# Every weight chunk fetched as two half-size transfers that signal one semaphore

## The chip, the cores and the metric

The kernel runs on one core of a Trainium2 chip. A core has TensorE (PE; its weight loads are listed as PEld), VectorE (DVE), ScalarE (ACT), GpSimd (POOL), and SyncE (SP), which in this kernel issues nearly all loads. Sixteen DMA engines move the data. The metric is the device time of one execution in microseconds; lower is better.

## The reference

Two blocks of two layers each, in f32, on 256 tokens (and 256 context tokens) of width 1024. The first block's layers are a modulated norm, an attention, and a mixture of experts; the second block's layers are attentions over latents and compressed keys, and a dense feed-forward of width 4096. What matters here is the weights that have to come in from HBM, and above all the experts:

```
def expert_block(args):
    xb, e = args
    return (jax.nn.silu(xb @ w1[e]) * (xb @ w3[e])) @ w2[e]
```

There are 32 experts in each of the two layers, w1 and w3 are 1024 x 512 and w2 is 512 x 1024 for each expert, so that one expert has 6 MiB of weights in f32, and one layer 192 MiB. The kernel fetches the weights of every expert, whatever the routing chose.

## The kernel before

**Chunks and places.** Weights come in chunks, mostly of 1 MiB: 128 partitions by 2048 floats, 8 KiB in each partition. `slot_at` names 20 places for a chunk: 6 in `ring`, and others in `rows`, `gate`, `arena`, `X` and `hT` at times when these hold nothing else. Each place has its own semaphore, `loaded[slot]`. SP runs the whole list of chunks in the order in which they are needed. For each it takes the next place (`Slots.take`), waits on the semaphore `used` until TensorE is done with the chunk that had the place before, and issues one DMA in `load` (line 3007), which adds 16 to `loaded[slot]` when it has landed. TensorE's `weights` (line 2168) waits for `loaded[slot]`, by a `Tally` that counts in units of 16.

**What a chunk is in HBM.** For w1 and w3 of an expert, partition p holds the rows 8p to 8p+7, each of 512 floats, and a chunk is four of these rows; for w2 it holds the rows 4p to 4p+3 of 1024 floats and a chunk is two of them. So each partition's 8 KiB of an expert chunk lie together in HBM, and the transfer is 128 pieces of 8 KiB, eight for each DMA engine. Chunks of `cols512` (the other projections, `w_mod`, `w_ff1_2`) are 4 x 128 pieces of 2 KiB, and chunks of `rows256` (`w_ff2_2`) are 2 x 128 pieces of 4 KiB.

**The experts.** `experts(l)` goes through 16 pairs of experts, 12 chunks to a pair: j = 0 to 3 are the chunks of w1, 4 to 7 those of w3, 8 to 11 those of w2 (even and odd expert in turn). The first pairs go to the places of `LEAD_PLACES`, all later ones to the 12 places of `STEADY_PLACES`, so 12 chunks are the most that are in flight or in use. Ahead of j = 11 of the first pair SP also stores the rows of the tokens (`h_rows`, line 3047), waits for the table that POOL scatters to HBM, loads it (line 3053), and waits until DVE has read it (`slots_ready`). For each further pair POOL gathers the tokens' rows with an indirect DMA (line 564), which moves on the same 16 DMA engines. On TensorE a pair is `up` twice (line 2689, w1 then w3), sums for the tokens of the pair before (line 2699), and the product with w2 (line 2730).

Of the kernel before, what the change touches and what calls it, by code (L numbers as in the profile page):

```python
# [170 lines left out]
def build(nc, t):  # L171
# [7 lines left out]
    with ctx:  # L179
# [3 lines left out]
        def sem(name):  # L183
            return ctx.enter_context(nc.semaphore(name))
# [129 lines left out]
        def slot_at(i):  # L314

            if i < RING:
                return ring[:, i, :]
            if i < 8:
                return rows[:, 2 * (i - RING):2 * (i - RING) + 2, :].rearrange("p a n -> p (a n)")
            if i < 10:  # L320
                return gate[:, i - 8, :, :].rearrange("p a n -> p (a n)")
            if i < 12:
                return arena[:, 12288 + CHUNK * (i - 10):12288 + CHUNK * (i - 9)]
            if i < 14:
                return X[:, 2 * (i - 12):2 * (i - 12) + 2, :].rearrange("p a n -> p (a n)")
            if i == 14:
                return hT[:, 4:8, :].rearrange("p a n -> p (a n)")
            at = {15: 10240, 16: 15360, 17: 6144, 18: 2048, 19: 4096}[i]
            return arena[:, at:at + CHUNK]
# [5 lines left out]
        loaded = [sem(f"loaded{i}") for i in range(20)]  # L335
# [257 lines left out]
        def _(act):  # L593
# [174 lines left out]
            def heads_ab():  # L768
                for j in range(12):
                    cols = slice(P * (j % 4), P * (j % 4) + P)  # L770
                    b = AB[j // 4]
                    act.wait_ge(mm_a, jobs.next())
                    bank = next_bank()
                    _, nq, q0 = b["q"]
                    inst = act.activation(qT[:, q0:q0 + nq, cols], bank[:, 0:P * nq].rearrange("p (h n) -> p h n", h=nq), ACT.Copy)
                    if b["k"]:
                        g0 = b["k"][1]
                        inst = act.activation(kD[:, g0:g0 + 2, cols], bank[:, 256:512].rearrange("p (g n) -> p g n", g=2), ACT.Copy)
                    inst.then_inc(a_free, 1)
                    act.wait_ge(a_free, so_far(a_free))  # L780
# [1352 lines left out]
        def _(pe):  # L2133
            v_done, a_done = Tally(v_free), Tally(a_free)
            fetched = [Tally(s, 16) for s in x_fetched]
            vi, ai, slots = [0], [0], Slots()
            chunk_in = [Tally(s, 16) for s in loaded]
            xn_in, rws, outs, picks = Tally(xn_ready), Tally(rows_ready), Tally(att_o), Tally(pick_ready)
            expd, tv, ta = Tally(att_e), Tally(att_tv), Tally(att_ta)
            mixed, choice, x_done = Tally(mod_row), Tally(chosen), Tally(x_tile)  # L2140
# [855 lines left out]
        def _(sp):  # L2996
# [3 lines left out]
            def load(src):  # L3000

                slot, before = slots.take()
                if before is not None:
                    freed.n = before + 1
                    sp.wait_ge(used, freed.value())
                dst = slot_at(slot)[:, 0:src.shape[1] * src.shape[2]].rearrange("p (k n) -> p k n", k=src.shape[1])
                sp.dma_start(dst, src).then_inc(loaded[slot], 16)

            def tokens():

# [3 lines left out]
            def matrix(w, cols, first=0):  # L3014
                for c in range(first, cols):
                    for src in cols512(w, c):
                        load(src)
# [7 lines left out]
            def experts(l):  # L3025

                def chunk(pair, j):

                    expert = bass.ds(2 * pair + j % 2, 1)
                    if j < 8:  # L3030
                        load(rows_of(t["w1" if j < 4 else "w3"][l, expert], KB, 4 * (j // 2 % 2), 4))
                    else:
                        load(rows_of(t["w2"][l, expert], 4, 2 * ((j - 8) // 2), 2))
# [189 lines left out]
```

## Time and profile before

| | |
|---|---|
| Median of 3 runs | 2365.07 us (2363.0 to 2366.71) |
| The profiled execution: its time | 2367.21 us |
| The profiled execution: its span | 2365.4 us |
| PE busy | 2205.4 us, 93% of the span |
| DVE busy | 957.6 us, 40% |
| Loads issued by SP and ACT | 595.26 MB, 64.3% of the 16 DMA engines' span |
| DMA, mean over the span | 255 GB/s |

The span is the time from the first to the last instruction. A share of busy time is an average over stages with different limits: DMA is busy 64% of the time because it is saturated in some stages and nearly idle in others. A row of the chain of work is one step on the way back from the last instruction to what released it.

### The profile page before, as it was taken

How to read it: one execution, taken by the hardware profiler on the slowest of the kernel's cores; microseconds unless marked ns; L12 is line 12 of the kernel's file. 1: busy time of each engine (PE TensorE's matmuls, PEld its weight loads, DVE VectorE, ACT ScalarE, POOL GpSimd, SP SyncE). 2: the span in 40 equal slices, each digit the busy share in tenths (PEclk: the TensorE clock that was granted, in tenths of full speed). 3: DMA queues.
4: the chain of work that ended last, by engine and by line, in shares of the span. 5: the costliest groups of instructions: out<-in, count | busy, mean ns of one | idle time of the engine just before them, and what ended most of it. 6: DMA issues, size and time to landing. Idle time of an engine off the chain costs nothing.

```text
span 2365.4 us, 25900 instructions
## 1 busy us (share of the span) xinstructions
PE 2205.4 (93%) x9574; PEld 1111.5 (47%) x9574; DVE 957.6 (40%) x1803; ACT 346.3 (15%) x941; POOL 158.4 (7%) x206
## 2 busy tenths in 40 slices
PE   6989999999999999989998888889999999999998
PEld 2436554333333344455333333334768744567843
DVE  3567433344333456273222222224630345561245
ACT  2006221000000010061000000001520001341000
POOL 1210002000000002030100000000000000000000
PEclk9999999999999999999999999999999999999999
DMA  9673348999999962206999999993324444504432
GB/s 374 244 277 145 126 178 321 420 421 421 421 421 421 422 233 71 71 1 232 382 420 420 421 421 421 421 409 121 124 71 144 150 171 136 181 25 133 163 143 98
DMA packets 150763, 602.98 MB, mean 255 GB/s; under 512 B 12660, under 2 KB 25716, under 8 KB 101136
## 3 DMA queue, kind: packets, MB, share of 16 engines
q1 hardware_dynamic: 145264, 595.26, 64.3%
q0 software_dynamic: 4736, 5.99, 0.7%
q8 instruction: 60, 0.98, 0.2%
q10 hardware_dynamic: 672, 0.49, 0.1%
q14 instruction: 31, 0.25, 0.0%
HBM read 606.89 MB, written 4.72 MB: 259 GB/s over the span
## 4 chain that ended last, share of the span: by engine, by line
PE 54%; DMA 29%; DVE 10%; issue 2%; POOL 2%; ACT 2%; SPq 1%; DVEq 0%; ACTq 0%; POOLq 0%
DMA ring<-in_w 14%; DMA arena<-in_w 13%; PE psum L2903 9%; PE psum L2262 9%; PE psum L2925 7%; PE psum L2689 7%; PE psum L2176 4%; PE psum L2784 4%; PE psum L2351 2%; PE psum L2730 2%; PE psum L2699 2%; DMA rows<-in_w 1%; POOL rstd L483 1%; PE psum L2431 1%; PE psum L2470 1%
## 5 line engine op out<-in xcount | busy, mean ns | idle before, releaser
L2689 PE MATMUL psum<-ring,arena 128*64 128x512 f32 x1440 | 326.5, 596 | 40.7 <-DMA ring<-in_w 38.8
L1689 DVE TENSOR_TENSOR X<-X,psum 128x512 f32<-128x512 f32 x192 | 131.9, 687 | 290.2 <-PE psum L2699 290.0
L2689 PEld LDWEIGHTS psum<-ring,arena 128*64 128x64 f32 x1440 | 105.8, 137 | 254.0 <-issue 243.5
L2262 PE MATMUL psum<-ring,hT 128*128 128x512 f32 x512 | 223.2, 593 | 1.9 <-DVE hT L1465 0.7
L2903 PE MATMUL psum<-hT,ring 128*128 128x256 f32 x1024 | 221.5, 379 | 2.6 <-DVE hT L1808 2.6
L2903 PEld LDWEIGHTS psum<-hT,ring 128*128 128x128 f32 x1024 | 194.4, 190 | 29.3 <-DVE hT L1808 3.0
L2699 PE MATMUL psum<-arena 128*128 128x512 f32 x384 | 178.3, 601 | 0.0
L2176 PE MATMUL psum<-con,arena 128*128 128x128 f32 (+1 forms) x848 | 123.7, 287 | 29.9 <-DVE arena L1776 10.6
L2262 PEld LDWEIGHTS psum<-ring,hT 128*128 128x128 f32 x512 | 95.8, 190 | 117.4 <-issue 115.1
L2176 PEld LDWEIGHTS psum<-con,arena 128*128 128x128 f32 (+1 forms) x848 | 96.7, 145 | 86.3 <-issue 25.0
L1776 DVE TENSOR_TENSOR arena<-psum,arena 128x512 f32<-128x512 f32 x32 | 33.8, 1058 | 209.2 <-PE psum L2689 209.2
L2730 PE MATMUL psum<-arena 128*64 128x512 f32 x488 | 112.3, 595 | 0.8 <-DVE arena L1780 0.8
L2699 PEld LDWEIGHTS psum<-arena 128*128 128x128 f32 x384 | 68.0, 190 | 88.1 <-issue 86.5
L2730 PE MATMUL psum<-gate,arena 128*64 128x512 f32 x232 | 105.1, 596 | 0.9 <-DVE arena L1780 0.9
L481 POOL TENSOR_SCALAR rstd<-sumsq 128x8 f32<-128x8 f32 (+3 forms) x44 | 10.7, 243 | 1372.8 <-ACT rows L618 419.8
L2784 PE MATMUL psum<-ring,hT 128*128 128x512 f32 (+2 forms) x256 | 94.6, 525 | 3.2 <-DVE gate L1930 2.7
L954 ACT ACTIVATE arena<-psum 128x512 f32<-128x512 f32 x32 | 19.1, 597 | 527.0 <-PE psum L2689 527.0
L2925 PE MATMUL psum<-ring,arena 128*128 128x512 f32 x192 | 88.1, 593 | 3.0 <-DVE arena L2012 3.0
L943 ACT ACTIVATE arena<-psum 128x512 f32<-128x512 f32 x64 | 38.2, 597 | 342.2 <-PE psum L2176 323.0
L2010 DVE TENSOR_SCALAR arena<-psum 128x512 f32<-128x512 f32 x16 | 11.1, 691 | 186.6 <-PE psum L2903 186.6
L2262 PE MATMUL psum<-arena,hT 128*128 128x512 f32 x192 | 84.3, 593 | 1.8 <-DVE hT L1115 1.8
L2689 PE MATMUL psum<-rows,arena 128*64 128x512 f32 x288 | 72.1, 592 | 0.0
(365 smaller groups left out, 2722.3 us busy)
## 6 DMA issues: line engine op xcount, KB each, us to landing
ring<-in_w SPq DMA_DIRECT2D x186, 1024.0 KB, 24.0
arena<-in_w SPq DMA_DIRECT2D x83, 1024.0 KB, 23.0
ring<-in_w_ff SPq DMA_DIRECT2D x64, 1024.0 KB, 5.9
rows<-in_w SPq DMA_DIRECT2D x50, 1024.0 KB, 23.8
ring<-in_w_mod SPq DMA_DIRECT2D x32, 1024.0 KB, 13.3
gate<-in_w SPq DMA_DIRECT2D x31, 1024.0 KB, 21.3
hT<-in_w SPq DMA_DIRECT2D x19, 1024.0 KB, 21.5
X<-in_w SPq DMA_DIRECT2D x15, 1024.0 KB, 24.2
```

What stands on the lines that cost most here:

```text
L943: act.activation(xgT[:, b, 4 * h:4 * h + 4, :], psum[:, 5 + h, :].rearrange("p (k n) -> p k n", k=4), ACT.Copy).then_inc(a_free, 1)
L1689: dve.tensor_tensor(x, x, bank, ALU.add).then_inc(v_free, 1)
L1776: dve.tensor_tensor(act_by_quarter, quarters(bank), quarters(siluG), ALU.mult).then_inc(v_free, 1)
L2176: return pe.transpose(out, in_, ident)
L2262: inst = pe.matmul(bank, hT[:, k, P * m:P * m + P], w[k], start=k == 0, stop=k == KB - 1)
L2351: inst = pe.matmul(bank, hT[:, 4 * h + i, P * m:P * m + P], w[c][:, i, :], start=i == 0, stop=i == 3)
L2689: inst = pe.matmul(out[64 * e:64 * e + 64, :], xgT[:, b, k, 64 * e:64 * e + 64], m, start=k == 0, stop=k == KB - 1)
L2699: pe.matmul(bank, shareT[:, m, :], ySlot[:, 512 * h:512 * h + 512], start=True, stop=True).then_inc(mm_v, 1)
L2730: inst = pe.matmul(outs[h][64 * e:64 * e + 64, :], actT[:, f, 64 * e:64 * e + 64], m, start=f == 0, stop=f == 3)
L2784: inst = pe.matmul(bank[:, 0:n], hT[:, k, P * m:P * m + P], w[k // 4][:, k % 4, :], start=k == 0, stop=k == KB - 1)
L2903: inst = pe.matmul(bank[:, SEQ * f:SEQ * f + SEQ], w[k][:, at:at + P], hT[:, k, 0:SEQ], start=k == 0, stop=k == KB - 1)
L2925: return pe.matmul(psum[:, PRODUCTS[n], :], a, b, start=i == 0, stop=i == 15)
```

## The change

`load` issues two DMAs in place of one. Each moves half of the chunk to its half of the same place, and both add 16 to the same semaphore, so TensorE's tally counts in units of 32 and waits until both have landed. A chunk with several rows to a partition is cut between its rows (for an expert chunk: 4 KiB and 4 KiB of each partition's 8 KiB), one with a single row to a partition (`w_kv_up_2`) in the middle of the row. The order of the chunks, their places and the wait for `used` are the same; the loads that don't go through `load` (tokens, parameters, the table, gates, the stores, and the rounds of `late`) are not touched.

```
-            chunk_in = [Tally(s, 16) for s in loaded]
+            chunk_in = [Tally(s, 32) for s in loaded]
...
                 if before is not None:
                     freed.n = before + 1
                     sp.wait_ge(used, freed.value())
+                k, n = src.shape[1:]
                 dst = slot_at(slot)[:, 0:src.shape[1] * src.shape[2]].rearrange("p (k n) -> p k n", k=src.shape[1])
-                sp.dma_start(dst, src).then_inc(loaded[slot], 16)
+                halves = [(slice(0, k // 2), slice(0, n)), (slice(k // 2, k), slice(0, n))]
+                if k == 1:
+                    halves = [(slice(0, 1), slice(0, n // 2)), (slice(0, 1), slice(n // 2, n))]
+                for r, c in halves:
+                    sp.dma_start(dst[:, r, c], src[:, r, c]).then_inc(loaded[slot], 16)
```

On SP, at the head of the loop over two pairs of experts, before: each row with DMA is one chunk of w1, and the register instructions between them work out its address and the value to wait for.

```order
L3061 ISA
L3007 ISA
L3007 DMA ring<-in_w 128x2048
L3005 REGISTER_ALU
L3007 ISA
L3007 DMA ring<-in_w 128x2048
L3005 REGISTER_ALU
```

The same place of SP after the change, the same two chunks.

```order
L3066 ISA
L3012 ISA
L3012 DMA ring<-in_w 128x1024
L3012 ISA
L3012 DMA ring<-in_w 128x1024
L3005 REGISTER_ALU
L3012 ISA
L3012 DMA ring<-in_w 128x1024
L3012 ISA
L3012 DMA ring<-in_w 128x1024
L3005 REGISTER_ALU
```

Each chunk has two DMAs of 128 pieces of 4 KiB where it had one of 128 pieces of 8 KiB, and for w1 one more register instruction; nothing has changed its place, and the instructions of the other engines are the same as before.

## Rows read from the trace of the kernel before

**Rows 1.** The page: busy times, and the span in 40 equal slices.

```profile
PE 2205.4 (93%) x9574; PEld 1111.5 (47%) x9574; DVE 957.6 (40%) x1803; ACT 346.3 (15%) x941; POOL 158.4 (7%) x206
...
DMA  9673348999999962206999999993324444504432
GB/s 374 244 277 145 126 178 321 420 421 421 421 421 421 422 233 71 71 1 232 382 420 420 421 421 421 421 409 121 124 71 144 150 171 136 181 25 133 163 143 98
```

**Rows 2.** Chain of work, both expert stages: start us, us, what.

```profile
381.36 14.03 DMA ring<-in_w
...
707.24 25.99 DMA ring<-in_w
733.37 3.68 PE psum L2689 x16
737.74 25.98 DMA ring<-in_w
...
1523.84 25.60 DMA arena<-in_w
1549.57 3.68 PE psum L2689 x16
1553.59 25.66 DMA arena<-in_w
```

**Rows 3.** Waits of PE on transfers, whole span: us in total, times, longest.

```profile
PE psum L2689 <- DMA ring<-in_w: 38.8, 38, 1.6
PE psum L2182 <- DMA ring<-in_w_mod: 14.6, 1, 14.6
...
PE psum L2689 <- DMA arena<-in_w: 10.0, 13, 1.0
...
PE psum L2689 <- DMA rows<-in_w: 0.8, 1, 0.8
```

**Rows 4.** Stretches: busy us of each engine, clock, DMA share, GB/s.

```profile
384.00:764.00 380.00, 368.11 (x1534) 134.62 (x1532) 148.25 (x197) 21.50 (x36) 23.79 (x25) 1.00 1.01 421
...
1142.00:1587.00 445.00, 399.12 (x1728) 141.70 (x1725) 99.74 (x148) 25.69 (x43) 23.37 (x24) 1.00 1.01 420
```

**Rows 5.** DMA packets at 800 to 830 us, expert chunks alone.

```profile
DMA packets 1734, 12.63 MB, mean 421 GB/s; under 512 B 192, under 2 KB 192, under 8 KB 192
...
q1 hardware_dynamic: 1733, 12.62, 101.1%
```

**Rows 6.** DMA packets at 1928 to 1932 us, chunks of w_ff2_2 alone.

```profile
DMA packets 422, 1.66 MB, mean 416 GB/s; under 512 B 16, under 2 KB 16, under 8 KB 422
...
q1 hardware_dynamic: 422, 1.66, 101.1%
```

**Rows 7.** DMA packets at 16 to 28 us, pieces of 2 KiB alone.

```profile
DMA packets 2349, 4.65 MB, mean 387 GB/s; under 512 B 80, under 2 KB 80, under 8 KB 2349
```

**Rows 8.** Shorter stretches: w_ff2_2 chunks, then expert chunks that follow idle DMA.

```profile
2308.50:2311.50 3.00, 3.00 (x9) 1.32 (x8) 2.90 (x5) 0.00 (x0) 0.00 (x0) 1.00 1.04 427
1103.00:1109.00 6.00, 5.39 (x40) 4.60 (x39) 1.73 (x4) 2.04 (x4) 0.00 (x0) 0.93 1.01 425
```

**Rows 9.** DMA issues, whole span: KB each, median us to landing.

```profile
ring<-in_w SPq DMA_DIRECT2D x186, 1024.0 KB, 24.0
...
ring<-in_w_in_c SPq DMA_DIRECT2D x12, 1024.0 KB, 6.6
...
ring<-in_w_out_c SPq DMA_DIRECT2D x4, 1024.0 KB, 5.0
```

**Rows 10.** SP in order of time, 500 to 531 us: issues of chunks.

```profile
500.72 0.84 SPq L3007 DMA_DIRECT2D ring<-in_w  x2
504.15 0.84 SPq L3007 DMA_DIRECT2D rows<-in_w  x2
511.46 0.33 SPq L3007 DMA_DIRECT2D gate<-in_w  x1
```

**Rows 11.** SP in order of time, start of layer 1's expert stage.

```profile
1096.45 1.28 SPq L3007 DMA_DIRECT2D ring<-in_w  x3
...
1131.74 0.33 SPq L3053 DMA_DIRECT2D arena<-slot_table  x1
1136.54 0.33 SPq L3007 DMA_DIRECT2D arena<-in_w  x1
```

**Rows 12.** Chain of work, last pairs of layer 0.

```profile
772.86 7.07 PE psum L2689 x32
...
802.78 7.07 PE psum L2689 x32
...
832.75 7.07 PE psum L2689 x32
```

**Rows 13.** Waits of SP, 384 to 1590 us.

```profile
SPq L3007 <- PE psum L2689: 394.4, 115, 7.8
```

**Rows 14.** Chain of work, start of the program.

```profile
13.29 14.62 DMA gate<-in_w_mod
27.91 2.80 issue
```

## The prediction

> **What bounds the kernel now.** I began with the page's slices. PE is busy 93% of the span, and yet in slices 8 to 14 and 20 to 27 the DMA engines are full, at a flat 420 to 422 GB/s [rows 1]. These are the two expert stages, and a flat top like this says that DMA may set the pace although PE is nearly always busy. The chain of work settles it. In layer 0 it has one wait of 26 us for a chunk in each pair of experts, with some 3.7 us of PE behind it, and the next such wait begins 30.5 us after the last (707.24 to 737.74) [rows 2]. In layer 1 the same goes on to 1553.59 + 25.66 = 1579.25 us. The 26 us are not the time of a transfer but of the queue ahead of it: the median chunk lands 24.0 us after its issue [rows 9], and a chunk takes some 2.49 us of all 16 engines (below), so about ten are queued. PE's own waits for these chunks are short, 38.8 + 10.0 + 0.8 us in all [rows 3], because the work of PE takes nearly as long as that of DMA: 368.11 of 380 us in layer 0, 399.12 of 445 us in layer 1 [rows 4]. So a longer chunk delays the end of an expert stage by nearly its full cost, and a shorter one would soon meet PE, above all in layer 0.
>
> Elsewhere PE waits for a transfer once, 14.6 us near the start [rows 3], where the queue is full too [rows 7, 14]. Nothing of the second block waits for a load.
>
> **What a 1 MiB chunk costs.** Three sizes of piece can be read, each in a stretch where the queue held nothing else. Time is stretch x 16 engines / data packets.
> - 8 KiB (experts before): 1734 packets in 30 us, 192 of them under 512 B (the writes to the semaphore, and a few more), so 30 x 16 / 1542 = 311 ns a piece [rows 5]. A chunk has 8 to an engine: 2.49 us.
> - 4 KiB: 422 packets in 4 us, 16 of them small, so 4 x 16 / 406 = 157.6 ns, and 16 to an engine make 2.52 us [rows 6].
> - 2 KiB: 2349 packets in 12 us, 80 small: 84.6 ns, and 32 to an engine make 2.71 us [rows 7].
>
> The middle one is what the change makes of an expert chunk, so by rows 5 and 6 the smaller pieces add 0.03 us. The second completion adds one small packet to each engine. Its price alone isn't in a row. Below, it is nothing, if it hides behind the data; above, I take what the line through the 2 and 8 KiB pieces leaves for a packet of no size, 84.6 - (311 - 84.6) / 3 = 9 ns. Together 0.04 us.
>
> How sure is this? From below: another stretch of 4 KiB pieces shows 427 GB/s in 3 us [rows 8], where whole packets at its edges weigh some 1%; if 4 KiB pieces ran at the 421 GB/s of the 8 KiB ones, only the completion would be left, 0.009 us. From above: the line through 2 and 8 KiB gives 84.6 + 75.5 = 160 ns for 4 KiB, a chunk of 2.56 us, and with the completion +0.08 to 0.09 us. One more comparison speaks for more: expert chunks that follow an idle queue run at 425 GB/s [rows 8], 2.47 us a chunk, and the 4 KiB rows are of that kind too; like with like the difference is 0.055 us, with the completion 0.06. I take 0.045 us, nearer to the longer stretches.
>
> The Trainium skill (DMA: Bandwidth & Descriptors, "Why small descriptors are slow (HBM only)") speaks against this change: each packet has a fixed overhead of about 3 cycles beside one cycle for 32 bytes. By that a chunk would grow from 8 x 259 to 16 x 131 cycles, 1.2%, an estimate of 0.03 us, and the time by some 10 us; this case's rows agree on the sign and leave the size between 0.009 and 0.09 us.
>
> **How many chunks it counts for.** In layer 0 the first pair comes piecemeal. SP works through the lead, and the chain turns to DMA at 381.36 us, with a chunk that lands at 395.39: j = 3 of the second pair, chunk number 15, since the chain repeats with each pair, and 737.74 + 25.98 = 763.72 is twelve pairs of 30.7 us later, chunk 159 [rows 2]. From 764 on the chain is PE's: the first products of a pair follow each other by 29.92 and 29.97 us [rows 12], and twelve chunks without gathers take 12 x 2.49 = 29.9 us. PE and DMA are level there to 0.1 us a pair; a slower DMA stays the limit until the last pair, chunk 183. From chunk 11 (the one that ends the idle time at about 378 us) to 183 are 172 to 173 chunks: 172 x 0.045 = 7.7 us, less 0.1 of slack.
>
> In layer 1 the queue fills at 1096 us [rows 11] and the lead counts as well: the table's load is issued at 1131.74 behind chunks still queued in the same queue, and what it releases begins at 1136.54. From chunk 3 to chunk 187 (j = 7 of the last pair, the last wait of the chain) are 185: 8.3 us. That PE has the chain up to 1187 us changes nothing, since the queue stays full beneath it at 420 GB/s [rows 4], and it is the queue that PE then meets.
>
> At the start seven chunks of `w_mod` precede the one wait [rows 14]. They have 2 KiB pieces before and after, so they gain only the completion: 7 x 0.009 = 0.1 us.
>
> **What costs nothing.** The other 160 or so chunks, behind PE's work: no wait of PE names them [rows 3], and one that lands 6.6 us after its issue [rows 9] would land a few hundredths later. Without that cover each would cost its 0.01 to 0.045 us, 7 us at most. SP issues twice as often. An issue takes 0.33 us and the two in a row 0.84 [rows 10], so 24 in a pair take 12 us of SP's 30.5. Behind a waiting issue stand all later loads, but SP waits for PE most of the time (394.4 us on line 2689 alone) [rows 13] and its issues run 24 us ahead of their landing. The second half is issued 0.5 us after the first, which needs 1.25 us to move, so no gap opens, not even for a lone chunk. There is no gain either: PE still waits for both halves, and nothing lands for it sooner.
>
> Sum: 7.7 - 0.1 + 8.3 + 0.1 = 16.0 us, 0.68%. The profiled execution took 2367.21 us, 1.8 more than its span; the median of the runs is 2365.07. The sum goes on the median: 2381 us.
>
> **The rivals.**
> - **Nothing to measure** (0.09): 4 KiB pieces cost the same for a byte as 8 KiB ones, as the 427 GB/s of rows 8 allow, and the completion hides or costs its 9 ns: 357 x 0.009 = 3 us, 2368. Against it: the 416 GB/s of rows 6, the longest such stretch.
> - **Twice the cost** (0.09): in the full queue, with HBM rows now 16 KiB apart and half used in each pass, a piece costs the line's 160 ns: 357 x 0.085 = 30 us, 2395. A kin of it is a shallower queue. If the queue held ten transfers and not ten chunks, it would hold 12.5 us of work. SP's longest wait in the stage is 7.8 us [rows 13], so it would still not run dry; only below three chunks would each pair lose time.
> - **Faster** (0.03): 4 KiB pieces stream better in the full queue than 8 KiB ones. The place is the queue in both stages, the price from the 427 GB/s: 2.456 us a chunk, and 9 ns more, 0.025 us less than now, so 357 x 0.025 = 9 us, 2356. (In layer 0 PE's 29.9 us a pair would stop part of it.) It decides once a 4 KiB piece takes under 155 ns.
> - **A fixed cost for each transfer that nothing hides** (0.01): a lone chunk takes 5 to 6.6 us to land [rows 9] against 2.49 in the stream, so about 2.5 us are latency. If a second transfer paid that in the queue, 357 x 2.5 = 890 us would come on top, 3260 us. The 8 KiB stream shows none of it between transfers at 421 GB/s and a share of 101.1% [rows 5]. The rule of the Trainium skill (DMA: Bandwidth & Descriptors, "Rules for kernel authors") to move at least 1 MiB in a DMA for full bandwidth would point this way, for transfers that don't overlap; rows 5 show them overlapped.
>
> **How the numbers follow.** My forecast (0.78) is 0.015 to 0.08 us a chunk, so 2370 to 2394. With the edge of the first rival the range is 2368 to 2395, which leaves out the last two rivals and the tails. About 0.2%, 4.7 us, is what a measurement here can tell from no change. That is 0.013 us a chunk. Slower by more: 0.78 + 0.09 + 0.01 = 0.88; within it: 0.09; faster: 0.03.
>
> **What would show it.** The packets in an expert stretch all at 4 KiB and twice as many; the rate there near 414 GB/s (421 x 2.49 / 2.535) with the share still at 101%; chunks 2.53 us apart and a pair of layer 0 at 31.0 us; PE's waits for chunks longer by some 15 us in sum, the last pairs of layer 0 waiting for DMA as well; the second block as long as before. It would be wrong if the rate stayed at 421, if the DMA share fell below 1.00 between issues, or if PE waited in the second block.

## The result and the profile after

| | |
|---|---|
| Median of 3 runs | 2392.40 us (2391.82 to 2392.50) |
| Before | 2365.07 us |
| Ratio | 1.0115, 95% interval 1.0101 to 1.0130 |
| The profiled execution: its time, its span | 2392.5 us, 2390.7 us |
| PE busy | 2203.2 us, 92% |

The changed kernel is slower by 27.3 us in the medians and by 25.3 us between the two profiled executions. The forecast was 16.0 us, so the direction and the place are as predicted and the size is too small by 40%. The measured time lies near the upper edge of the stated range, 2368 to 2395.

The page of the changed kernel, busy tenths and GB/s in 40 slices, answers to [rows 1]:

```profile
PE 2203.2 (92%) x9574; PEld 1107.5 (46%) x9574; DVE 958.2 (40%) x1803; ACT 346.4 (14%) x941; POOL 158.5 (7%) x206
...
DMA  9673348999999972205999999994424443503442
GB/s 374 248 261 146 124 178 324 408 409 409 409 409 409 410 270 76 70 1 204 381 408 409 409 409 409 409 407 148 159 71 141 141 176 132 185 15 131 168 145 97
```

The flat top of both expert stages is still flat, at 409 GB/s where it was 421. The stretches of the same kernel (busy us of each engine, clock, DMA share, GB/s) say the same, and answer to [rows 4]:

```profile
384.00:764.00 380.00, 358.45 (x1490) 131.96 (x1489) 143.94 (x191) 21.82 (x37) 24.29 (x25) 1.00 1.03 409
...
800.00:830.00 30.00, 29.10 (x122) 10.66 (x120) 11.45 (x16) 1.79 (x3) 0.00 (x0) 1.00 1.03 410
```

The DMA engines are no less busy than before, 1.03 against 1.01, and move less. So no gap has opened; the packets themselves take longer for a byte. The packets of the changed kernel at 800 to 830 us, the stretch of [rows 5]:

```profile
DMA packets 3371, 12.29 MB, mean 410 GB/s; under 512 B 372, under 2 KB 372, under 8 KB 3371
...
q1 hardware_dynamic: 3371, 12.29, 102.6%
```

By the prediction's own formula a piece of 4 KiB takes 30 x 16 / (3371 - 372) = 160.0 ns here, and a chunk 16 x 160.0 = 2.561 us. Before it was 2.490 us [rows 5]: 0.071 us more for each chunk.

The chain of work of the changed kernel (start us, us, what) answers to [rows 2, 12]:

```profile
540.20 16.02 DMA ring<-in_w
565.36 7.07 PE psum L2689 x32
602.99 16.63 DMA ring<-in_w
...
822.96 15.51 DMA ring<-in_w
847.60 7.07 PE psum L2689 x32
```

From 540.20 to 602.99 are two pairs, 31.4 us each, where a pair took 30.5 us in [rows 2]. (A single pair's distance varies by half a microsecond. From landing to landing in the chain, ten pairs of the changed kernel take 31.50 us each (430.20 to 745.22) and eleven of the kernel before 30.64 (426.70 to 763.72), so that a chunk takes 0.072 us more.) The last pairs of layer 0, which were PE's before [rows 12], wait for DMA too: the product that began at 832.75 us now begins at 847.60, 14.85 us later. Following the same instruction of PE through both traces, it is 2.2 us late at 354 us (ahead of the experts), 14.8 at 828, 14.5 at 1112, 27.1 at 1579 and 25.3 at the end. Each expert stage adds 12.6 us, and what lies between adds nothing. The 2 us at the start and the 2 us that come back behind 1579 are of a kind that other runs show with either sign: in the run below that halves only the other chunks, PE is 0.7 us early at 354 and 3.7 us early at the end.

PE's waits on transfers in the changed kernel (us in total, times, longest), against 38.8, 14.6, 10.0 and 0.8 in [rows 3]:

```profile
PE psum L2689 <- DMA ring<-in_w: 58.6, 43, 1.8
PE psum L2182 <- DMA ring<-in_w_mod: 14.7, 1, 14.7
PE psum L2689 <- DMA arena<-in_w: 14.1, 13, 1.5
...
PE psum L2689 <- DMA rows<-in_w: 1.1, 1, 1.1
```

The waits for expert chunks (ring, arena and rows) are 24.2 us longer, and that accounts for nearly all of the 25.3 us.

One thing looks quite different and costs nothing. The issues of the changed kernel (KB each, median us to landing) and its issuing line (duration ns, shortest, median, longest):

```profile
ring<-in_w SPq DMA_DIRECT2D x372, 512.0 KB, 15.0
```

```profile
L3012 SPq DMA_DIRECT2D ring<-in_w x372: 327/937/4177, 303.6 to 1585.8; - x186
```

A transfer lands 15.0 us after its issue, where a whole chunk took 24.0 [rows 9], and the median issue takes 937 ns where one alone took 0.33 us [rows 10]. At 1.28 us for each transfer, about 15.0 / 1.28 = 12 of them are queued (an estimate), six chunks' worth where it was ten chunks, and SP now stands in front of a full queue and hardly waits on PE's line 2689 any more (4.4 us, 394.4 before [rows 13]). The chain therefore shows 9% of SP's queue and 16 us waits. Neither is the cause: the rate stays flat and the DMA share at 1.03, so the queue never ran dry.

### The profile page after: what moved, and what is told of

The parts are those of the page before. It is cut to its first block, busy times and chain, and to the rows that moved or that the text cites. A ratio compares the mean times of both kernels' runs of the same rounds, so it can differ in the third digit from the quotient of the medians.

```text
span 2390.7 us, 26842 instructions
## 1 busy us (share of the span) xinstructions
PE 2203.2 (92%) x9574; PEld 1107.5 (46%) x9574; DVE 958.2 (40%) x1803; ACT 346.4 (14%) x941; POOL 158.5 (7%) x206
## 4 chain that ended last, share of the span: by engine, by line
PE 60%; DMA 14%; DVE 11%; SPq 9%; issue 2%; ACT 2%; POOL 1%; DVEq 0%; ACTq 0%; POOLq 0%
PE psum L2262 9%; PE psum L2903 9%; SPq L3012 9%; PE psum L2689 7%; PE psum L2925 7%; DMA arena<-in_w 7%; DMA ring<-in_w 6%; PE psum L2730 5%; PE psum L2176 4%; PE psum L2784 4%; PE psum L2699 4%; PE psum L2351 2%; POOL rstd L483 1%; PE psum L2431 1%; PE psum L2470 1%
```

## The experiments

**The price of a piece by itself: the queue with nothing behind it.** A kernel that only loads. SP issues 24 expert chunks (16 for `w_ff2_2`) in each stage, at most 12 chunks ahead; nothing is computed. This kernel and the two of its kind below ran once each.

```
if form == "whole8":
    return [(dst, src)]
if form == "halves4":
    return [(dst[:, 0:h // 2], src[:, 0:h // 2]), (dst[:, h // 2:h], src[:, h // 2:h])]
if form == "parts8":
    return [(dst[0:64], src[0:64]), (dst[64:128], src[64:128])]
if form == "strided4":
    src = w.rearrange("(p a c b) n -> p a c (b n)", a=2, c=2, b=h // 2)[:, :, part, :]
```

> Nothing is computed: SP alone streams weights into 12 places of one tile, in ten stages with the queue drained between them. Stages 1 to 7 are 24 expert chunks each: whole (8 KiB pieces), halves (as changed), one transfer with 4 KiB pieces that lie 16 KiB apart in HBM, one transfer with 4 KiB pieces that adjoin in HBM, two transfers of 64 partitions with 8 KiB pieces, whole with at most 4 chunks in flight, halves with at most 4; then 12 transfers of 2 MiB with 16 KiB pieces, then 16 chunks of w_ff2_2 whole (4 KiB pieces) and 16 in halves. Before, a chunk in the full queue took 2.485 us of all engines and after the change 2.56. Theory 'pieces' (each packet has a fixed part of some 8 ns, the completion 7 to 9): the three forms with 4 KiB pieces take 2.53 to 2.56 us a chunk and differ by no more than the completion, 64 partitions cost under 0.02 more than whole, 16 KiB pieces save 0.03. Theory 'transfers' (the boundary between two transfers costs some 70 ns): halves and the 64-partition form are slow, the single transfers with 4 KiB pieces as fast as whole. Theory 'stride' (HBM rows half used in a pass): adjoining pieces are as fast as whole, the others not. Theory 'full queue': at 4 chunks in flight each chunk takes 0.03 us less than at 12, in both forms.

Stretches inside each stage of this kernel (POOL's busy time, clock, DMA share, GB/s). In order: whole, halves, one transfer of 4 KiB pieces, one transfer of 4 KiB pieces that adjoin in HBM with 128 bytes between them in SBUF, two halves by partitions, whole with 4 in flight, halves with 4 in flight, 16 KiB pieces in 2 MiB transfers, `w_ff2_2` whole, `w_ff2_2` in halves.

```profile
10.00:59.00 49.00, 0.00 (x0) 1.00 1.01 423
72.00:124.00 52.00, 0.00 (x0) 1.00 1.03 410
138.00:192.00 54.00, 0.00 (x0) 1.00 1.03 409
205.00:254.00 49.00, 0.00 (x0) 1.00 1.02 420
268.00:371.00 103.00, 0.00 (x0) 1.00 1.02 219
385.00:434.00 49.00, 0.00 (x0) 1.00 1.01 422
448.00:499.00 51.00, 0.00 (x0) 1.00 1.03 410
513.00:561.00 48.00, 0.00 (x0) 1.00 1.00 429
575.00:605.00 30.00, 0.00 (x0) 1.00 1.03 410
618.00:648.00 30.00, 0.00 (x0) 1.00 1.03 410
```

The bare queue repeats the kernel's numbers, 423 against 410 GB/s: 1048.6 / 423 = 2.479 and 1048.6 / 410 = 2.557 us a chunk, 0.078 more. Two transfers that each cover 128 partitions are no worse than one with the same pieces (410 and 409), `w_ff2_2` costs the same whole or halved since its pieces of 4 KiB become no smaller, and 4 chunks in flight do as well as 12. At 429 GB/s a piece of 16 KiB takes 16 x 16384 / 429 = 611 ns. So the size of the piece decides, and neither the number of these transfers nor the depth. The fourth row didn't fit: 4 KiB pieces at 420 GB/s. It differs in two things from the third, in HBM and in SBUF, and is taken up below.

The same stages also show why the prediction under-read the price. Packets of the first stage, whole chunks of 8 KiB pieces, at 4 to 12 us, and at 30 to 60 us:

```profile
DMA packets 464, 3.41 MB, mean 426 GB/s; under 512 B 48, under 2 KB 48, under 8 KB 48
```

```profile
DMA packets 1736, 12.64 MB, mean 421 GB/s; under 512 B 193, under 2 KB 193, under 8 KB 193
```

An 8 KiB piece takes 8 x 16 / 416 = 307.7 ns in the first microseconds and 30 x 16 / 1543 = 311.1 ns later. The ninth stage, `w_ff2_2` in 4 KiB pieces, does the same, here at 571 to 579 us and at 580 to 604 us:

```profile
DMA packets 858, 3.32 MB, mean 415 GB/s; under 512 B 48, under 2 KB 48, under 8 KB 858
```

```profile
DMA packets 2548, 9.83 MB, mean 410 GB/s; under 512 B 148, under 2 KB 148, under 8 KB 2548
```

8 x 16 / 810 = 158.0 ns early and 24 x 16 / 2400 = 160.0 ns later. The first microseconds after an idle queue are 1% cheap, and the 4 us of [rows 6], 157.6 ns, are of that kind. (The stage of halves can't be read there: a dip to some 200 GB/s lies in its first microseconds.) Early against early, a chunk costs 16 x 158.0 - 8 x 307.7 = 0.066 us more, late against late 16 x 160.0 - 8 x 311.1 = 0.071; early 4 KiB pieces against late 8 KiB ones, as [rows 5, 6] had them, give only 0.039 (with the 157.6 ns of the prediction, 0.03).

**One transfer, the same pieces.** The kernel before with one transfer for each chunk, of 4 KiB pieces: a chunk takes every other 4 KiB of each partition's rows, and TensorE takes the rows in the order in which they now lie.

```
-                    load(rows_of(t["w1" if j < 4 else "w3"][l, expert], KB, 4 * (j // 2 % 2), 4))
+                    w, part = (t["w1" if j < 4 else "w3"], j // 2 % 2) if j < 8 else (t["w2"], (j - 8) // 2)
+                    load(w[l, expert].rearrange("o (p a c b) n -> p (o a) c (b n)", a=2, c=2, b=2 if j < 8 else 1)[:, :, part, :])
```

> The kernel before, one transfer a chunk, but the expert chunks take rows 0, 1, 4, 5 (or 2, 3, 6, 7) of a partition's eight, and rows 0, 2 or 1, 3 of w2's four, so that the pieces are 4 KiB; TensorE takes its left operands in the same order. The same is computed. Theory 'pieces' or 'stride': 2.55 us a chunk, 349 chunks x 0.066 = 23 us more than before, 2388. Theory 'transfers': within 2 us of before.

It took 2391.54 us (2390.41 to 2392.72), 1.0116 (1.0099 to 1.0132) times the kernel before: the whole loss of the change without a second transfer. Its packets at 800 to 830 us:

```profile
DMA packets 3188, 12.29 MB, mean 410 GB/s; under 512 B 188, under 2 KB 188, under 8 KB 3188
```

3188 - 188 = 3000 data packets, where the change has 3371 - 372 = 2999 in the same time. The change writes to semaphores twice as often and moves as many pieces. In the longer stretch from 420 to 740 us it moves 31,930 pieces of data and this kernel 31,942, so the second completion costs at most some 0.001 us a chunk.

This kernel also shows that the queue isn't limited to 12 transfers as such. A transfer has 16 pieces for each engine here, lands 19.2 us after its issue, and its issue takes 2152 ns in the median: 19.2 / 2.56 = 7.5 transfers are queued. In pieces for each engine that is 120, where the change has 15.0 / 0.160 = 94 and the quarters below have 8.5 / 0.0847 = 100 (estimates, with the latency counted in). What the limit counts wasn't tested.

**Two transfers, the same pieces.** The counterpart: each chunk is cut between partitions 63 and 64, so that the pieces stay at 8 KiB.

```
-                for r, c in halves:
-                    sp.dma_start(dst[:, r, c], src[:, r, c]).then_inc(loaded[slot], 16)
+                for r in (slice(0, 64), slice(64, 128)):
+                    sp.dma_start(dst[r], src[r]).then_inc(loaded[slot], 16)
```

> Two transfers a chunk as in the change, but cut by partitions (0 to 63, 64 to 127), so that the pieces stay 8 KiB and only completions and transfers double. Theory 'pieces': 349 x 0.007 to 0.009 = 2.4 to 3 us more than before, 2368. Theory 'transfers': as the change, 25 us more, 2390. A third possibility: 64 partitions are spread over the engines in another way, and rates fall for that reason; the stream of the same form would show it without compute.

It took 3075.15 us (2964.31 to 3110.95), so even the fastest of its four executions is 600 us slower than the kernel before. The packets at 500 to 700 us:

```profile
DMA packets 7369, 45.42 MB, mean 227 GB/s; under 512 B 1718, under 2 KB 1718, under 8 KB 1934
```

The pieces are whole and the rate is about half, as in the fifth row of the bare queue (219 GB/s, share 1.02). A transfer into 64 partitions has a limit of its own, which no row here explains, so this run doesn't test what it was made for. The run before it does.

**Only the others.** Expert chunks whole, all other chunks of `load` in halves.

```
-                        load(rows_of(t["w1" if j < 4 else "w3"][l, expert], KB, 4 * (j // 2 % 2), 4))
+                        load(rows_of(t["w1" if j < 4 else "w3"][l, expert], KB, 4 * (j // 2 % 2), 4), True)
...
+                if whole:
+                    sp.dma_start(dst, src).then_inc(loaded[slot], 32)
+                    return
```

> The change for every chunk but the experts', which stay one transfer (adding 32 to its semaphore). All theories: these chunks lie behind PE's work, 2364 to 2367 us. If it is over 2370, part of the loss is outside the expert stages.

2363.92 us (2362.38 to 2367.51), a ratio of 1.000 (0.9991 to 1.0010). Outside the expert stages the change costs nothing.

**One layer at a time.** The same switch, with every chunk whole except the expert chunks of layer 0 in one kernel and of layer 1 in the other.

```
+                        load(rows_of(t["w1" if j < 4 else "w3"][l, expert], KB, 4 * (j // 2 % 2), 4), l == 1)
```

> Only the expert chunks of layer 0 come as two halves; every other chunk comes whole, with an increment of 32. If the chunk cost adds up over the chunks in front of which the queue is full, as the shifts of PE's instructions in the profile of the change say (12.6 us gained by the end of layer 0's stage), it takes 12 to 13 us more than the kernel before: 2376 to 2378 us. Reason for the sum being smaller in one layer: PE and DMA are level in layer 0 (29.95 us a pair against 29.9), so the rival has layer 0 losing less than its half, 9 to 11 us, with the rest in layer 1.

> The counterpart: only the expert chunks of layer 1 come as two halves. The adding-up theory expects 12 to 13 us more than the kernel before, 2376 to 2378 us, the two runs together the 27 us of the change (177 chunks at 0.072 us are 12.7 us). If the lead of layer 1 counted, as the prediction had it, it would be 185 chunks, 13.3 us, with TensorE's instructions already later when the first product of the stage begins; if it doesn't, nothing is later by more than 0.3 us at the end of the lead.

They took 2376.78 us (1.0055, 1.0041 to 1.0069) and 2376.95 us (1.0061, 1.0047 to 1.0075), against 2363.41 us: 13.4 and 13.5 us, together 26.9 of the change's 27.3. The costs add, and layer 0 pays as much as layer 1 although PE and DMA were level in its last pairs. The stretches of the kernel with layer 0 in halves, then of the one with layer 1 in halves:

```profile
384.00:764.00 380.00, 357.89 (x1485) 131.81 (x1482) 142.67 (x190) 21.51 (x36) 23.28 (x24) 1.00 1.03 408
1250.00:1560.00 310.00, 274.42 (x1184) 97.57 (x1182) 68.78 (x102) 18.52 (x31) 17.56 (x18) 1.00 1.01 421
```

```profile
384.00:764.00 380.00, 367.88 (x1532) 134.52 (x1530) 147.90 (x196) 21.50 (x36) 23.35 (x24) 1.00 1.01 421
1250.00:1560.00 310.00, 266.69 (x1152) 94.64 (x1148) 67.36 (x100) 17.91 (x30) 17.52 (x18) 1.00 1.03 409
```

Each stage takes its own rate, whatever the other does. In the second kernel the same instruction of PE is 0.3 us late at 1112 us, 1.4 at 1201, and 12.9 at 1600.

**A quarter in place of a half.** Expert chunks in four transfers of 2 KiB pieces, all others whole.

```
+                if k == 2:
+                    dst, src = (x.rearrange("p k (a n) -> p (k a) n", a=2) for x in (dst, src))
+                for i in range(4):
+                    sp.dma_start(dst[:, i:i + 1], src[:, i:i + 1]).then_inc(loaded[slot], 16)
```

> Only the experts' chunks are cut, each into four transfers with pieces of 2 KiB; all others are whole. By the price of a piece in the full queue (2 KiB pieces before: 2.71 us a chunk with one completion, three more at 7 to 9 ns): 2.73 us, 0.245 more than before, on 349 chunks 86 us, 2450. If a transfer of its own cost what only the change's two halves hid, or SP's 48 issues a pair (0.5 us each, 24 of 33 us) came to bind, it is more, over 2480.

2448.58 us (2447.12 to 2450.04), 1.0353 (1.0334 to 1.0372) times before, 85.0 us more. The packets at 800 to 830 us:

```profile
DMA packets 6375, 11.60 MB, mean 387 GB/s; under 512 B 710, under 2 KB 710, under 8 KB 6375
```

30 x 16 / (6375 - 710) = 84.7 ns a piece, 32 x 84.7 = 2.711 us a chunk, 0.221 more than whole. The three sizes lie on one line: 84.7, 160.0 and 311 ns, 75.5 ns for each 2 KiB and 9 ns for the packet. A 16 KiB piece lies on it too: the line gives 613 ns, the bare queue had 611. The prediction had drawn this line, with 160 ns on it, and taken it for the upper bound.

**A piece in place of two.** The kernel before, with a pair's 8 MiB of w1 and w3 (four matrices of 2 MiB) loaded as far as the places allow in 2 MiB transfers of 16 KiB pieces (all four matrices in layer 0, three in layer 1).

```
+                            dst = (rows[:, :, :] if first == RING else ring[:, first:first + 2, :]).rearrange("p a n -> p (a n)")
+                            sp.dma_start(dst, w.rearrange("o (p k) n -> p (o k n)", k=KB)).then_inc(loaded[first], 16)
```

> The other way: in the steady pairs of both layers an expert's w1 (and w3, but in layer 1 only that of the even expert) comes as one transfer of 2 MiB with 16 KiB pieces into two places that adjoin; the first pairs, the last pair and w2 stay as before. The first stream had 2.443 us per MiB against 2.479 for 8 KiB pieces. Theory 'pieces': 14 pairs of layer 0 save 8 x 0.036 each and 10 of layer 1 save 6 x 0.036, 6.2 us in all, if PE, which then waits for four chunks before the first product, doesn't hold the places too long; 2359. Rival: PE is level with DMA in layer 0 (29.95 against 30.5 us a pair), and starts 3.5 us later in each pair: no gain or a loss, 2364 to 2370.

2362.55 us (2360.43 to 2365.42) against 2363.59, a ratio of 0.9991 (0.9982 to 1.0000). Its stretch in layer 0:

```profile
420.00:740.00 320.00, 315.03 (x1311) 115.35 (x1311) 127.54 (x170) 18.51 (x31) 20.71 (x22) 1.00 1.01 425
```

The rate rises to 425 GB/s and PE is busy 315.0 of 320 us (311.0 of 320 before). PE falls 6 us behind at its first such pairs (at 391 us in layer 0, 1262 in layer 1), since it waits for a matrix to land whole, and has made that up by the end of the stage. In this trace layer 0's stage ends 0.7 us earlier against its start than before, of 4.0 us that the pieces alone would save, and layer 1's 2.3 us earlier, of 2.2. So larger pieces do give back time, and in layer 0 PE takes it. From 1250 to 1270 us, a stretch with such a wait of 6 us, the granted clock of TensorE was 0.83 of full speed on average, where it was 1.00 before. The version isn't clearly better than the kernel before.

**What made the one stage fast.** The bare queue again, 24 chunks in each stage. In order: 4 KiB pieces that don't adjoin in HBM, with 128 bytes between them in SBUF; the same with none; adjoining in HBM, with 128 bytes, 4 KiB and 32 bytes between them in SBUF; 2 KiB pieces that adjoin, 64 bytes between; 2 KiB pieces that don't.

```
stage(list(strided(2, 1056)))
stage(list(strided(2, 1024)))
stage(list(adjacent(2, 1056)))
stage(list(adjacent(2, 2048, 4096)), 6)
stage(list(adjacent(2, 1032)))
stage(list(adjacent(4, 528)))
stage(list(strided(4, 512)))
```

> Nothing is computed; stages of the same kind as the first stream, 24 chunks of w1 and w3 each. The first stream had 4 KiB pieces at 2.56 us a chunk in three forms, but at 2.49 where the two pieces of a partition adjoin in HBM; there the second piece also lay 128 bytes further on in SBUF. Stages: (1) pieces of 4 KiB apart in HBM, with that gap in SBUF; (2) the same without it; (3) adjoining in HBM, gap 128 bytes; (4) adjoining, gap 4 KiB; (5) adjoining, gap 32 bytes; (6) 2 KiB pieces, four adjoining, gaps of 64 bytes; (7) 2 KiB pieces apart in HBM; (8) whole chunks, an expert's two halves one after the other; (9) whole chunks in the kernel's order; (10) 2 MiB transfers of two adjoining 8 KiB pieces. Theory 'HBM': pieces that adjoin cost nearly nothing, whatever the gap: (1) = (2) = 2.56, (3) = (4) = (5) = 2.49. Theory 'SBUF': the gap does it: (1) = (3) = 2.49, (2) = 2.56. By the first, (6) is near 2.55 and (7) at 2.71 or more, (10) at 2.45.

The stretches of these seven stages:

```profile
10.00:64.00 54.00, 0.00 (x0) 1.00 1.02 416
77.00:131.00 54.00, 0.00 (x0) 1.00 1.02 409
144.00:194.00 50.00, 0.00 (x0) 1.00 1.03 420
207.00:258.00 51.00, 0.00 (x0) 1.00 1.03 410
272.00:323.00 51.00, 0.00 (x0) 1.00 1.03 410
336.00:389.00 53.00, 0.00 (x0) 1.00 1.05 398
402.00:456.00 54.00, 0.00 (x0) 1.00 1.05 387
```

Not a gap as such (32 bytes and 4 KiB do nothing for 4 KiB pieces) and hardly HBM (416 against 420), but 128 bytes in SBUF make the difference. The sixth row, 398 GB/s with gaps of 64 bytes against 387, differs from the seventh in two things, and which of them helps wasn't separated. The kernel's last three stages, (8) to (10), all ran at 423 GB/s: whole chunks in either order, and 2 MiB transfers of two 8 KiB pieces each. The last had been expected at 2.45 us for 1 MiB and took 2.48, so a larger transfer gains nothing if its pieces stay as they are. So the address itself was suspected, and tested with whole chunks too. Places apart by 8192 bytes and 0, 32, 128, 384, 512, 1024 and 2048 more, then halves with the second 4224, 4096 and 4608 bytes behind the first:

```
for n, pitch in enumerate((2048, 2056, 2080, 2144, 2176, 2304, 2560)):
    stage(list(whole_at(pitch)))
for n, (pitch, second) in enumerate(((2112, 1056), (2048, 1024), (2304, 1152))):
    stage(list(halves_at(pitch, second)))
```

> Nothing is computed. In the second stream a gap of 128 bytes between a partition's two 4 KiB pieces in SBUF took 0.04 to 0.06 us off a chunk, whether the pieces adjoined in HBM or not, and gaps of 32 bytes or 4 KiB did not. Stages of 24 chunks: whole chunks (8 KiB pieces) with places 0, 32, 128, 384, 512, 1024 and 2048 bytes apart, then halves with places and gaps of 8448 and 4224, 8192 and 4096, 9216 and 4608 bytes. Theory 'addresses' (a packet costs some 4 ns more in a long stream where the destinations of neighbouring packets have unlucky distances): some spacing of the whole chunks streams at 2.45 us a chunk and the others at 2.48, and a place spacing in the kernel could gain up to 349 x 0.03 = 10 us. Theory 'one transfer' (only the gap inside one transfer does it, since it splits the access in another way): all whole stages at 2.48, all halves at 2.56.

```profile
10.00:59.00 49.00, 0.00 (x0) 1.00 1.01 423
72.00:121.00 49.00, 0.00 (x0) 1.00 1.01 424
134.00:183.00 49.00, 0.00 (x0) 1.00 1.01 428
196.00:245.00 49.00, 0.00 (x0) 1.00 1.01 428
258.00:307.00 49.00, 0.00 (x0) 1.00 1.01 423
321.00:370.00 49.00, 0.00 (x0) 1.00 1.01 423
383.00:433.00 50.00, 0.00 (x0) 1.00 1.01 423
446.00:497.00 51.00, 0.00 (x0) 1.00 1.03 420
510.00:561.00 51.00, 0.00 (x0) 1.00 1.03 410
575.00:626.00 51.00, 0.00 (x0) 1.00 1.03 411
```

These are the stretches of the ten stages. Where each destination differs from the one before by an odd multiple of 128 bytes, whole chunks run at 428 and halves at 420 GB/s; elsewhere at 423 or 424 and 410. (The others that were tried are 32 bytes and multiples of 512; an even multiple such as 256 wasn't.) Of the 13 GB/s that the change loses, 10 come back in the bare queue by moving the addresses, but whole chunks gain 5 by it too.

**The addresses in the kernel.** Nine small tensors (128 or 384 bytes) moved in between the places, so that 10 of 12 chunks of layer 0 and 7 or 8 of 12 of layer 1 differ so from the one before, once in the kernel before and once in the changed one. In the latter the second half of a chunk still lies 4096 bytes behind the first, so that only 10 of 24 transfers differ in layer 0 and 7 or 8 in layer 1.

```
-        ring = sb("ring", [P, RING, CHUNK])
+        ring, small = [], []
+        for i, (name, shape) in enumerate((("scale1", [P, 2, KB, 2]), ("gain", [P, 2, KB, 2]), ("nbias", [P, 4, 8]),
+                                           ("psums", [P, 4, 8]), ("esink", [P, 4, 8]), ("rden", [P, 4, 8]))):
+            ring.append(sb(f"ring{i}", [P, CHUNK])[:, :])
+            small.append(sb(name, shape))
```

> The kernel before, with whole chunks, and only the addresses in SBUF changed: nine small tensors that lay behind the arena (128 or 384 bytes in each partition) now lie between the six places of the ring and between X, hT, gate, rows and arena. So in layer 0's expert stage 10 of 12 chunks, and in layer 1's 7 or 8 of 12, have a destination that differs from the one before by an odd multiple of 128 bytes. The theory of addresses (a packet stays at 309 ns where neighbouring destinations differ so, and rises to 313 elsewhere in the full queue; in the stream alone 2.455 against 2.480 us a chunk) expects 172 x 0.025 x 10/12 = 3.6 us in layer 0, less where PE's 29.95 us a pair stops it, and 177 x 0.025 x 8/12 = 3 us in layer 1: 2357 to 2361 us, with 423 to 426 GB/s in the expert stages. The rival, that the effect belongs to the bare stream, or needs every neighbour to differ, expects the time of the kernel before, 2362 to 2366 us, and 420 to 422 GB/s.

> The changed kernel (two transfers for a chunk) with the same addresses as in the run padded. The halves of a chunk lie 4096 bytes apart, so only every second transfer changes by an odd multiple of 128 bytes, about 10 of 24 in layer 0 and 8 of 24 in layer 1. If the gain goes by the share of neighbouring transfers that differ, a chunk wins 0.06 x 10/24 = 0.025 us and 0.02 us, 172 x 0.025 + 177 x 0.02 = 8 us: 2384 us, 412 to 413 GB/s. If every neighbour has to differ, it is 2392 us as the change, 409 GB/s. If one different neighbour in a chunk is enough, it is 20 us less, 2372 us, 418 GB/s.

The kernel before with these addresses took 2367.32 us (1.0011, 1.0002 to 1.0020), the changed one 2388.70 us (1.0103, 1.0088 to 1.0119), both against 2364.92 us. A stretch of each:

```profile
420.00:740.00 320.00, 310.77 (x1291) 113.82 (x1288) 123.42 (x165) 18.51 (x31) 19.46 (x20) 1.00 1.01 421
```

```profile
420.00:740.00 320.00, 303.70 (x1264) 111.42 (x1262) 122.03 (x163) 17.93 (x30) 19.50 (x20) 1.00 1.03 409
```

421 and 409 GB/s, as without it, and the first version is even 2.4 us slower, for a reason that wasn't looked for. A gain by the share of differing neighbours, which would have given 2357 to 2361 and 2384 us, falls: what holds in a queue in which every neighbour differs gives nothing where most do. Whether all must differ, or the gathers and PE's reads undo it, stays open; no version of the kernel with all twelve places apart was tried.

## Why the prediction was right in sign and place, and short in size

- **DMA sets the pace of both expert stages, and a longer chunk delays their end by nearly its full cost.** Right. PE's waits for expert chunks grew by 24.2 of 25.3 us, the two layers alone cost 13.4 and 13.5 us, and the last pairs of layer 0 turned from PE's into DMA's.
- **A 4 KiB piece costs 157.6 ns, a chunk 0.045 us more.** This step failed: the term was mis-sized. In the full queue the piece takes 160.0 ns, the chunk costs 0.071 us more by its packets, 0.072 by the pairs of the chain ((31.50 - 30.64) / 12), and 27.3 / 349 = 0.078 by the median. The value was taken "nearer to the longer stretches" of 4 KiB pieces, but these were 3 and 4 us long and soon behind an idle queue [rows 6, 8], where pieces are 1% cheap, compared with 8 KiB pieces of a full one [rows 5]. The text had the comparison of like with like (both behind an idle queue), 0.055 us, and the line through 2 and 8 KiB pieces in full queues, 160 ns, and took neither for its value. The line was exact, and it is what kept the range wide enough.
- **The second completion costs up to 0.009 us.** Too high; it hides. With one transfer for each chunk the time was 2391.54 us, with two 2392.40, and the data packets in 320 us were 31,942 and 31,930. The Trainium skill (DMA: Bandwidth & Descriptors, "Anatomy of one DMA — SWDGE (gpsimd) path") calls the write to the semaphore nearly free on trn2, there for GpSimd's path; these counts agree for SP's. So the mis-sized piece is the error, and the share of the completion in the 0.045 us hid part of it.
- **172 and 185 chunks.** No run speaks against 172. In layer 1 the lead was counted too, and it doesn't count: the issue of the table's load moved from 1131.74 [rows 11] to 1146.32 us and the next chunk's from 1136.54 to 1151.28, 14.6 and 14.7 us, no more than the 14.8 brought along from layer 0, and with only layer 1 in halves PE is 0.3 us late at 1112 us and not at all at 1180. About 177 chunks are left. This error went the other way, by 8 x 0.045 = 0.4 us.
- **Nothing behind the experts, nothing on SP, no harm from a shallower queue.** Right in time. With the others alone in halves the ratio is 1.000. SP wasn't left as it was, though: it stands in front of the queue where its issues had run 24 us ahead. Depth fell to about 12 transfers, as the kin of the second rival had it, and as it also said, the stage never ran dry; in the bare queue even 4 chunks in flight kept 422 and 410 GB/s.
- **The rivals.** The time of "twice the cost", 2395 us, lies nearer to 2392.40 than the forecast does, and of its parts the line's 160 ns is what happened; pieces that lie apart in HBM count for little (409 against 410 GB/s, 416 against 420 with 128 bytes between). The rival of a fixed cost for each transfer is refuted. By the fixed part of a packet that the Trainium skill gives (DMA: Bandwidth & Descriptors, "Why small descriptors are slow (HBM only)"), a chunk would cost 0.03 us more, an estimate; the runs have 0.07 to 0.08, so the sign agrees and the measurement decides on the size.

The sum of the packets, redone with these numbers, is 349 x 0.071 = 24.8 us. Measured are 27.3 us with an interval from 23.9 to 30.7, so the two agree. For the quarters it is 349 x 0.221 = 77 us against 85.0 (79 to 88), and here the count has grown: in the trace of the quarters PE is 41.1 us late at 1112 us and 45.3 at 1180, ahead of the first chunk that the chain of the kernel before names in layer 1 (1187.36). Chunks this slow make the lead of layer 1 count after all. That is 4.2 of the 8 us; the rest isn't separated.

## What to carry to other kernels

When a queue is full, read a piece's price from a stretch in which the queue has been full for long, and compare full with full; where the size in question has no such stretch, the line through two sizes that have one is better than a short stretch behind an idle queue. Splitting a transfer costs nothing by itself, if the pieces in each partition keep their size and each transfer still covers all 128 partitions (two transfers of 64 partitions each ran at half the rate): what is paid is the number of pieces, some 9 ns each on its DMA engine, and only where the queue sets the pace. A larger piece wins the same amount back, but in a kernel where the compute engine is busy for 97% of the queue's time it wins almost nothing.

## What the runs showed of the hardware

- Pieces of 2, 4, 8 KiB in the full queue take 84.7, 160.0 and 311 ns; 16 KiB pieces give 429 GB/s in the bare queue, 611 ns each.
- Soon after an idle queue they are 1% cheaper: 307.7 against 311.1 ns, and 158.0 against 160.0.
- Transfers into 64 partitions move 219 GB/s, with all 16 DMA engines shown busy (share 1.02), against 423 into 128. I had expected equal rates.
- In the bare queue destinations in SBUF that differ by an odd multiple of 128 bytes from one transfer to the next give 428 against 423 GB/s for 8 KiB pieces and 420 against 410 for 4 KiB. In the kernel, where 7 to 10 of 12 chunks differed, they gave nothing.
- About 12 transfers of 512 KB are queued (landing 15.0 us after the issue at 1.28 us each), but only 7 to 8 of 1 MB in pieces of 4 KiB (19.2 us at 2.56). SP's issue then waits, 937 ns in the median in the first case and 2152 in the second, where an issue into a queue with room takes 333.
